# Expert stage of a one-layer inference step: two u units kept at the opening, V products over three banks, coefficient and gathered rows between the V products

## The reference

```python
t1, i1 = lax.top_k(s1, PEER_TOPK)          # and t2, i2: keys of 128 x 128 experts
...
u = jnp.take(u_tab, ib, axis=0)            # 128 experts of each token
h = jax.nn.gelu(jnp.einsum('nkd,nd->nk', u, xb), approximate=False)
vv = jnp.take(v_tab, ib, axis=0)
return jnp.einsum('nk,nkd->nd', gb * h, vv)
```

## Time and profile before

| what | value |
| --- | --- |
| median of 3 runs | 5207.31 us (5204.38 to 5211.70) |
| the profiled execution's own time | 5207.63 us |
| its span | 5205.5 us |
| PE busy | 4768.7 us, 92% |
| DVE busy | 2992.9 us, 57% |
| POOL busy | 2332.6 us, 45% |
| ACT busy | 1394.0 us, 27% |
| first loop / turn / main loop begin at | 2929.6 / 3171.3 / 3259.6 us of the span |
| main loop ends at | 5148.3 us |

### The profile page before, as it was taken

The page is one execution under the profiler, slowest core; times in us unless marked ns, Lnnn a source line. Parts: engine busy times, 40 slices in busy tenths (PEclk is TensorE's granted clock), DMA queues, the critical chain, the costliest instruction groups (busy, mean ns, idle before and its releaser), DMA issues. The chain is left out here.

```text
span 5205.5 us, 91321 instructions
## 1 busy us (share of the span) xinstructions
PE 4768.7 (92%) x35388; PEld 4590.3 (88%) x35388; DVE 2992.9 (57%) x4978; ACT 1394.0 (27%) x1809; POOL 2332.6 (45%) x892
## 2 busy tenths in 40 slices
PE   6999899999999799969788799999999999999998
PEld 5999788888888798969778799999999999999997
DVE  4333255555555432359988564666666666666665
ACT  3333212222222221121233232222222222222222
POOL 3222212221221133332322354777777777777874
PEclk8999999999999899989899898999999999999999
DMA  6999633333333277931234555677777777777773
GB/s 234 335 335 336 243 120 107 125 125 115 125 116 125 66 238 287 325 108 64 84 120 181 201 162 178 244 273 255 266 265 254 266 245 270 254 268 263 266 265 119
DMA packets 338640, 1070.23 MB, mean 206 GB/s; under 512 B 98833, under 2 KB 148497, under 8 KB 259345
## 3 DMA queue, kind: packets, MB, share of 16 engines
q1 hardware_dynamic: 286656, 776.20, 44.0%
q0 software_dynamic: 36864, 268.45, 13.6%
q10 hardware_dynamic: 14928, 22.84, 1.2%
HBM read 873.50 MB, written 193.88 MB: 205 GB/s over the span
## 5 line engine op out<-in xcount | busy, mean ns | idle before, releaser
L154 POOL TENSOR_TENSOR wlo<-raw,whi 128x2048 fp32r<-128x2048 f32 x156 | 718.9, 4610 | 2150.5 <-ACT whi L150 2150.5
L168 POOL TENSOR_TENSOR wlo<-raw,whi 128x1024 fp32r<-128x1024 f32 x460 | 1248.1, 2713 | 560.1 <-ACT whi L164 556.7
L164 ACT ACTIVATE whi<-raw 128x1024 fp32r<-128x1024 f32 x460 | 487.6, 1060 | 1177.1 <-PE psR L236 647.3
L2092 DVE TENSOR_TENSOR H<-psR,H 128x416 f32<-128x416 f32 x832 | 487.1, 590 | 437.0 <-PE psR L236 430.4
L236 PE MATMUL psR<-chi,whi 128*128 128x416 f32 x1664 | 591.8, 356 | 58.8 <-DVE H L2092 57.6
L236 PE MATMUL accs<-xh,whi 128*128 128x272 f32 x2624 | 580.6, 303 | 68.4 <-DMA at_before<-in_cst 40.6
L236 PE MATMUL psS<-hh,whi 128*128 128x416 f32 x1664 | 585.0, 352 | 4.7 <-DVE clo L2081 4.7
L236 PE MATMUL psR<-chi,wlo 128*128 128x416 f32 x1664 | 589.0, 354 | 0.0
L236 PE MATMUL psS<-hh,wlo 128*128 128x416 f32 x1664 | 587.9, 353 | 0.0
L236 PE MATMUL psR<-clo,whi 128*128 128x416 f32 x1664 | 584.5, 351 | 0.0
L236 PE MATMUL psS<-hl,whi 128*128 128x416 f32 x1664 | 582.5, 350 | 0.0
(11 more groups left out here) (380 smaller groups left out, 8758.2 us busy)
## 6 DMA issues: line engine op xcount, KB each, us to landing
raw<-in_u SPq DMA_DIRECT2D x128, 1024.0 KB, 9.4
raw<-in_v SPq DMA_DIRECT2D x128, 1024.0 KB, 5.8
raw<-in_w_in SPq DMA_DIRECT2D x82, 1024.0 KB, 8.7
at_UI<-in_u SPq DMA_DIRECT2D x64, 1024.0 KB, 8.9
u_d<-at_UO SPq DMA_DIRECT2D x256, 256.0 KB, 6.2
g_d<-STG SPq DMA_DIRECT2D x8, 3328.0 KB, 10.3
Ge<-g_d SPq DMA_DIRECT2D x64, 416.0 KB, 10.3
wo_UI<-in_u SPq DMA_DIRECT2D x24, 1024.0 KB, 9.2
```

The lines of the kernel that those rows point to most:

```text
L154: pool.tensor_tensor(self.lo[:, c % 2, :], self.raw[:, c % 2, :], self.hi[:, c % 2, :].bitcast(F32), ALU.subtract).then_inc(self.split_don ...
L164: act.activation(self.half(self.hi, c, h), self.half(self.raw, c, h), ACT.Copy).then_inc(self.hi_done, 1)
L168: pool.tensor_tensor(self.half(self.lo, c, h), self.half(self.raw, c, h), self.half(self.hi, c, h).bitcast(F32), ALU.subtract).then_inc(se ...
L2092: dve.tensor_tensor(h, v_bank(d, per), h, ALU.add).then_inc(S["ex_added"], 1)
```

## The change

The count of u units made ahead goes from 24 to 28: TAIL is 10, and START = 2 units are multiplied by PE at the very opening of `experts`, into the banks of `psR`; ACT's Gelu puts them into the third buffer of `R`, SP stores them to `pre_d`, and they are read back with the last kept group. FIRST becomes 14. The V products of the main loop turn over three banks, the third being the first u bank; PE therefore waits before V product 2 for the first coefficient's low part, and before the next u pair for the add of V product 14. A period has six rows: one dot, up to three sum rows, then dots; row 4 is done after add 4, row 5 after add 9. The second coefficient's scale and low part come in the same period, around the first two adds, and no longer in the next one. POOL gives its gathers behind the halves, and two of the six between the halves of the u units. The factors of the dots are made at the period's end.

```diff
-TAIL = 8
-PRE = TAIL + 2 * GB_N
+TAIL = 10
+START = 2
+PRE = TAIL + 2 * GB_N + START
...
-        v_bank = lambda d, per: psR[:, d % 2, 0:TD] if per == N else accs[:, d % 4, 0:TD]
+        v_banks = [psR[:, 0, 0:TD], psR[:, 1, 0:TD], psS[:, 0, 0:TD]]
+        v_bank = lambda d, per: v_banks[d % 3] if per == N else accs[:, d % 4, 0:TD]
+        early = R[:, 2, 0:2 * TD].rearrange("p (k t) -> p k t", k=2)
...
-            known = dotted
-            nv = min(known - summed, 2 + j % 2 if dotted < P else 5)
-            nu = min(5 - nv, P - dotted)
+            in_u, in_v = 4, 2 if j else 0
+            nv = min(dotted - summed, 3 if dotted < P else in_u + in_v)
+            nu = min(in_u + in_v - nv, P - dotted)
+            us, vs = [("u", dotted + n) for n in range(nu)], [("v", summed + n) for n in range(nv)]
+            order = us[:1] + vs + us[1:]
+            phases.append((order[:in_u], order[in_u:], len(gathers)))
...
@@ block.sync
+            for h in range(2):
+                v_unit(2 + h, 0, 0, h)
+            for k in range(START):
+                sp.wait_ge(S["ex_early"], k + 1)
+                sp.dma_start(row(pre_d, PRE - START + k), early[:, k, :]).then_inc(S["ex_early_kept"], 16)
...
@@ block.gpsimd
-            for g in range(FIRST, GROUPS - 1):
-
-                c = C0 + 2 + 4 * (g - FIRST) + 2
-                gather(1)
-                lo(c, 0)
-                gather(1)
-                lo(c, 1)
-                gather(1)
-                lo(c + 1, 0)
-                gather(1)
-                lo(c + 1, 1)
-                gather(1)
-                for n in range(2):
-                    for h in range(2):
-                        lo(c + 2 + n, h)
+            for j, (in_u, in_v, _) in enumerate(phases):
+                c = C0 + 2 if j == 0 else C0 + 4 * j
+                for h in range(4):
+                    lo(c + h // 2, h % 2)
+                    gather(1 if h < len(in_u) else 0)
+                if j == 0:
+                    continue
+                lo(c + 2, 0)
+                gather(1 if in_v else 0)
+                lo(c + 2, 1)
+                lo(c + 3, 0)
+                gather(len(in_v) - 1 if in_v else 0)
+                lo(c + 3, 1)
...
@@ block.tensor
+                    if c % 2 == 0:
+                        pe.wait_ge(S["ex_added"], 8 * count - 13)
...
-                    pe.wait_ge(S["ex_added"], n + (3 if per == N else 1))
+                    if per == N and at == 2 and not (isinstance(group, int) and group == GROUPS - 1):
+                        pe.wait_ge(S["ex_coef"], 2 * group + 5)
+                    pe.wait_ge(S["ex_added"], n + 1 if per != N else n + 2 if at >= 3 else n - at + 4)
...
+            for k in range(START):
+                u_products(k, 0)
...
@@ block.scalar
+                if c < START:
+                    W.wait_used(act, c)
+                    act.activation(early[:, c, :], psR[:, c, 0:TD], ACT.Gelu).then_inc(S["ex_early"], 1)
...
-                coef_hi(2 * g + 1)
                 unit_done(c, True)
-                if g == FIRST:
-                    gather_gelu(0)
                 coef_hi(2 * g + 2)
                 unit_done(c + 1, True)
+                coef_hi(2 * g + 3)
                 unit_done(c + 2)
+                unit_done(c + 3)
                 gather_gelu(g + 1 - FIRST)
...
@@ block.vector
-                scale(2 * g + 1)
-                rows_of(j, 0, 1)
-                coef_lo(2 * g + 1)
-                rows_of(j, 1, 3)
+                rows_of(j, 0, 3)
                 scale(2 * g + 2)
                 rows_of(j, 3, 4)
                 coef_lo(2 * g + 2)
+                scale(2 * g + 3)
+                add(0, c + 2, g, to=2)
+                coef_lo(2 * g + 3)
+                add(0, c + 2, g, at=2, to=5)
                 rows_of(j, 4, 5)
-                add(0, c + 2, g)
-                add(1, c + 3, g)
+                add(0, c + 2, g, at=5)
+                add(1, c + 3, g, to=2)
+                rows_of(j, 5, 6)
+                add(1, c + 3, g, at=2)
```

More of the change, by code:

```diff
@@ L264, in build @@
         W = Stream(S, sball("raw", [P, 2, D]), sball("whi", [P, 2, D], F32R), sball("wlo", [P, 2, D], F32R))
-        counts = {"attention": 4 * HEADS, "rwkv": 6 * PAIRS + 2, "mix": KB, "out": KB, "retrieval": 2 * PH + TAIL, "gates": PRE - TAIL}
+        counts = {"attention": 4 * HEADS, "rwkv": 6 * PAIRS + 2, "mix": KB, "out": KB, "retrieval": 2 * PH + TAIL, "gates": 2 * GB_N}
         base, at = {}, 0
@@ L1807, in experts @@
         for j in range(GROUPS - FIRST):
-            known = dotted
-            nv = min(known - summed, 2 + j % 2 if dotted < P else 5)
-            nu = min(5 - nv, P - dotted)
-            phases.append((dotted, nu, summed, nv, len(gathers)))
-            gathers += [("v", summed + n) for n in range(nv)] + [("u", dotted + n) for n in range(nu)]
+            in_u, in_v = 4, 2 if j else 0
[4 more added lines that the diff above has]
+            phases.append((order[:in_u], order[in_u:], len(gathers)))
+            gathers += order
             dotted, summed = dotted + nu, summed + nv
@@ L2019, in gather_gelu @@
             def gather_gelu(j):
-                s, n, _, nv, at = phases[j]
-                if n:
-                    act.wait_ge(S["gx_done"], GBUF + at + nv + n)
+                dots = [x for kind, x in phases[j][0] + phases[j][1] if kind == "u"]
+                if dots:
+                    s, n = dots[0], len(dots)
+                    act.wait_ge(S["gx_done"], GBUF + gathers.index(("u", dots[-1])) + 1)
                     act.activation(HD[:, s:s + n], HD[:, s:s + n], ACT.Gelu).then_inc(S["gx_gelu"], 1)
@@ L2041, in _ @@
                         coef_hi(count)
-                unit_done(2 * g)
-                unit_done(2 * g + 1)
+                unit_done(START + 2 * g)
+                unit_done(START + 2 * g + 1)
             unit_done(C0, True)
@@ L2081, in coef_lo, with add @@
                 dve.tensor_tensor(clo[:, par, k, :], u_bank(count), chi[:, par, k, :].bitcast(F32), ALU.subtract).then_inc(S["ex_coef"], 1)
-            def add(half, c, group, per=N):
-                for d in range(8):
+            def add(half, c, group, per=N, at=0, to=8):
+                for d in range(at, to):
                     if per != N and d % 4 == 0:
@@ L2091, in add @@
                     h = H[:, 8 * half + d, 0:TD]
-                    dve.tensor_tensor(h, v_bank(d, per), h, ALU.add).then_inc(S["ex_added"], 1)
+                    dve.tensor_tensor(h, v_bank(8 * half + d, per), h, ALU.add).then_inc(S["ex_added"], 1)
             def rows_of(j, a, b):
-                s, nu, t, nv, at = phases[j]
-                for m in range(a, min(b, nu + nv)):
+                in_u, in_v, at = phases[j]
+                for m, (kind, x) in list(enumerate(in_u + in_v))[a:b]:
                     n = at + m
@@ L2105, in rows_of @@
                     else:
-                        x = t + m
-                        if m == 0:
-                            dve.wait_ge(S["gx_coef"], 1 + max(p for p in range(j) if phases[p][1] and phases[p][0] <= t + nv - 1))
+                        dve.wait_ge(S["gx_coef"], 1 + next(p for p in range(j) if ("u", x) in phases[p][0] + phases[p][1]))
                         if x == 0:
@@ L2125, in _ @@
                 for h in range(2):
-                    add(h, 2 * g + h, g, 4)
+                    add(h, START + 2 * g + h, g, 4)
             scale(PRE)
```

53 lines of the change are left out of this document (24 added, 29 removed).

## The result

The changed kernel takes 5128.0 us (median of four runs, 5120.9 to 5132.7) against 5209.5 us (four runs, 5204.4 to 5223.4): ratio 0.983, 95% interval 0.981 to 0.985. Faster by 1.7%; the forecast was 5146 us. The profiled execution took 5132.1 us with a span of 5130.3, 75.2 less than the span before.

The account below looks back on a forecast made before the run. Main-loop bound: a gather's landing, passed through a DVE row and two banks, stalls PE. Terms 37 + 12 + 12 - 6 - 1 - 116 = -62 us from 5207.6 gave 5146 us, range 5112 to 5194.

Parts of the forecast that it names:

- First loop: Expert stage's first loop, V products alone: two more groups move there from the main loop, +37 us.
- Turn: Stretch into the main loop: second coefficient made before the sum rows, -6 us (-8 to 0).
- First V group: First V group, reckoned with the turn into the main loop: loses 1 us of its stall.
- TAIL: End of the retrieval stage: two more u units, 18.1 us of work, 6 hidden: +12 us (+9 to +18.1).
- Opening: Expert stage's opening: two u products before V, SP's store waits delay group 1's gate block: +12 us (+7.5 to +15.5).
- Main loop: 50 periods become 48 of 36.26 us, 40 of them losing 0.8 us: 1772.5 against 1888.7 us, -116 us.
- (b): Main loop's V products: dots of rows 4 and 5 between adds delay later products, 0.5 us a period.
- (c): Main loop, V product 2: row 3's gather and POOL's split may delay it, 0.3 us a period (0 to 1.5).
- Row 3 and the amid rows cost nothing: Rival, main loop: only 0.1 us a period lost, 28 us better, 5118 us; chance 0.15.
- The stall moves: Rival, main loop: row 3 lands late, V product 2 waits 1.5 us; 2.0 a period, 5194 us; chance 0.2.
- DMA too full: Rival, main loop: gathers land 2.5 us later, 4.2 us a period lost, 5282 us, slower; chance 0.1.
- The estimate of 5218 us: Main loop: every gather could land 1.8 us later at high DMA load, row 3 at 20.3 us at worst.

Follow-up runs that it names:

- e4: Changed kernel with the main loop's V products over two banks instead of three: main loop +123 us, whole kernel 5254.4 us (one run).
- e10: Changed kernel with row 4 moved back before the V products: main loop +232 us.
- e11: Changed kernel with each period's first three gathers asked for one split later on POOL's queue: main loop +284 us.
- e1: Changed kernel with 6 u units at the end of retrieval instead of 10: retrieval -16.6 us, expert stage +34.6, together +18 us.
- e3: Changed kernel with no u units in the opening and 12 at the end of retrieval: retrieval +17.1 us, expert stage -6.5, +10.5 in all.
- e5: Changed kernel with each first-loop group's coefficient loads and gate block one step earlier on SP's queue: V product 4 5.6 us earlier, median 5128.0 us.
- e12: Changed kernel with one more 1 MB DRAM to DRAM transfer a period issued by SP: main loop +5.0 us.
- e7: Changed kernel with the two dots amid the V products done in halves, joined by a 128x1 DVE add: main loop +20.6 us, median 5158.2 us.

## Why the prediction was right, and where it was off

- **What bounds the kernel.** Right: with the third bank PE's waits of the earlier trace rows are gone (0.11 us idle in the main loop). e4 brings them back by the bank, e10 and e11 by a row that comes late ahead of product 2.
- **First loop**, +37: +36.4. **Turn**, -6: -6.5 (68.3 to 61.8); the 4.7 us wait is gone. **First V group**, -1: -1.0.
- **TAIL**, +12 (9 to 18.1): +12.0 in the retrieval stage. The chain named is there: POOL's last half was put at 2637.0, which is 2643.8 with this execution's stage begun 6.8 us later, and ended at 2643.71; e1 to e3 show the price rise from 4.6 to the full 18 us.

```profile
2639.21 4.50 POOL L154 TENSOR_TENSOR wlo<-raw,whi 128x2048 fp32r<-128x2048 f32 x1 [4.45 <-ACT whi L150]
```

- **Opening**, +12 (7.5 to 15.5): +7.3, just outside. The chain was right, store by store: the gate block was put at 23.4 us from the stage's start and went out at 23.5. The term that was mis-sized is its load: the list's median of 10.3 us was taken, and it needed 5.4. The prediction's reason for the median, "other loads run beside it", had been true of the old opening; the new one moves the gate block behind most of them (e3, e5).
- **Main loop**, -116: -127.3. Of the 0.8 us a period, (b) was 0.5 and is 0.53, at products 8 and 13, as written. (c), 0.3 us for row 3, is 0. Its gather went out at 8.5 us and was held up by a sum row until 10.4, as reckoned; from there it landed in 5.4 us (15.9), where the rows of before had given 7.4 to 8.1. Why it was quicker is open. That POOL's split holds the row until 17.4, just inside the 17.5 that product 2 allows, was forecast to 0.1 us. 40 x 0.27 us makes the 11 us.
- **The sum.** -62 forecast, -75.2 in the spans of the two profiled executions: main loop -11 and opening -5 beyond it, first loop and turn -1 together, and -1 in the last V group, which also turns over three banks and was left out. The rest, -2 in the gate matrix and +7 ahead of retrieval, is the difference of two executions in stages that the change hardly touches. The two mis-sized terms err the same way, so nothing in the hit is owed to errors that cancel.
- **Rivals.** "Row 3 and the amid rows cost nothing" was half right (5118; row 3 only). "The stall moves" wanted 1.5 us at product 2: there is none, with 0.26 us to spare. "DMA too full" falls for this kernel: at 298 GB/s and a share of 0.82 row 3 landed in time in every period. Its mechanism is real elsewhere: in e12 gathers beside the extra transfer did land up to 2.3 us later. Its price was not overdrawn: e10 and e11 lose 5.8 and 7.1 us a period once product 2 is 4.1 and 4.5 us late, where the rival reckoned 4.2 for 2.7.
- **The estimate of 5218 us.** It took 1.8 us more for every gather from the Trainium skill's 2 us at high load ("DMA: Bandwidth & Descriptors", "Latency and other measured facts"). In the changed kernel row 3 landed between 15.7 and 16.9 us into the period, where that estimate has 20.3 at worst. The 2.3 us of e12 are of that size, but they are a wait beside one transfer of 1 MB, and no run tells access time from queueing.

## What to carry to other kernels

A buffer more on the consumer's side and a reordered filler belong together: the order alone, on two banks, costs more than the change gains, and three banks leave only what one filler exceeds the slack by (cutting the filler in two removed that). Price a moved load by what will run beside it in its new place, not by its median in the old one, and a stop of some us by the slow clock behind it as well as by its length. Before putting even a tiny operation between two critical ones, ask which port it needs: one element a partition cost 2.09 us. And when a median is to show that a load costs nothing, look at the transfers that run beside it one by one.

## What was not expected of the hardware

- A 128x1 DVE add with both inputs in SBUF took 0.15 us alone and 2.09 us beside a POOL split (e7).
- The shortest landing of a gather was 4.3 to 4.4 us after the end of POOL's instruction, whether that took 0.95 or 2.83 us; most in the changed kernel took 7.4 to 7.8 us from its start, and one in each period 10.1 beside the extra transfer of e12.
- A gate block of 416 KB took 13.4, 13.7 and 15.5 us beside H's rows and 5.4 us when they were nearly all in.
- After stops of 3.9 (e10), 4.4 (e11) and 6.2 us (changed kernel) PE ran at a granted clock of 0.50 (the 1.2 GHz level) for the next 10, 18 and 12 matmuls; the restarts after stops of 0.5 to 1.1 us in e4, e5 and e7 did not.
